# Expert lists: empty places alternate with used ones, a ring of four experts' weights, and gathers that leave out the rows of nobody

## The reference

```python
def _hier_moe(xn, w_rg, b_rg, w_re, b_re, w_gate, w_up, w_down):
    ...
    g_idx = jnp.argmax(g_logit, axis=-1)                  # one of 4 groups
    ...
    top_v, top_i = lax.top_k(e_sel, TOP_K_INNER)          # 2 of the group's 4 experts
    w_pair = jax.nn.softmax(top_v, axis=-1) * g_w
    expert_id = g_idx[..., None] * EXPERTS_PER_GROUP + top_i
    ...
    h = jax.nn.silu(jnp.einsum("btd,edf->btef", xn, w_gate)) * jnp.einsum("btd,edf->btef", xn, w_up)
    h = h * gates[..., None].astype(h.dtype)
    return jnp.einsum("btef,efd->btd", h, w_down)
```

## Time and profile before

| | us |
|---|---|
| median of the 2 runs | 1463.34 |
| lowest, highest | 1461.02, 1465.66 |
| the profiled execution | 1457.58 |
| its span (first to last instruction) | 1455.9 |
| PE busy in the span | 1147.6 (79%) |
| mean granted clock of PE | 0.887 |

### The profile page before, as it was taken

One profiled execution on the slowest core, in us unless ns is written; L12 is line 12 of the kernel. 1 busy time (PEld: TensorE's weight loads), 2 busy tenths in 40 slices (PEclk: granted clock), 3 DMA queues, 4 the chain that ended last, 5 costly groups with the idle time before them and its releaser, 6 DMA issues. The chain is left out here.

```text
span 1455.9 us, 24335 instructions
## 1 busy us (share of the span) xinstructions
PE 1147.6 (79%) x9100; PEld 866.7 (60%) x9100; DVE 574.3 (39%) x1014; ACT 468.4 (32%) x885; POOL 248.6 (17%) x290
## 2 busy tenths in 40 slices
PE   4699999498988979168687875899929979999940
PEld 3699999386877868145465554777624434444410
DVE  5320120253636455677777873212151211222231
ACT  6111010245444454467667744212100101111121
POOL 4100000000000000332323222222010221222231
PEclk9999999799898989678888887999958999999975
DMA  4402310221212020699898974932223899997567
GB/s 126 116 23 67 88 31 0 60 75 46 88 45 88 30 85 20 215 347 321 290 315 284 311 237 164 312 121 102 66 69 119 235 272 280 283 288 234 141 148 193
DMA packets 161696, 230.55 MB, mean 158 GB/s; under 512 B 15921, under 2 KB 104498, under 8 KB 161522
## 3 DMA queue, kind: packets, MB, share of 16 engines
q1 hardware_dynamic: 144962, 174.20, 36.4%
q0 software_dynamic: 13568, 49.03, 13.0%
q10 hardware_dynamic: 3072, 6.03, 1.1%
HBM read 184.13 MB, written 49.55 MB: 161 GB/s over the span
## 5 line engine op out<-in xcount | busy, mean ns | idle before, releaser
L2171 PE MATMUL ps<-ring,e_xgT 128*128 x400 | 180.7, 606 | 11.3 <-SPq L2092 10.2
L2171 PEld LDWEIGHTS ps<-ring,e_xgT 128*128 128x128 f32 x400 | 75.8, 195 | 98.9 <-issue 98.9
L634 PE MATMUL ps<-xh,a_wh 128*128 128x384 f32 (+1 forms) x288 | 101.1, 351 | 0.0
L634 PE MATMUL ps<-xl,a_wh 128*128 128x384 f32 (+1 forms) x288 | 97.1, 337 | 0.0
L634 PE MATMUL ps<-xh,a_wl 128*128 128x384 f32 (+1 forms) x288 | 96.8, 336 | 0.0
L2123 POOL DMA_INDIRECT y_rows<-e_oE,slot_to x32 | 50.5, 1579 | 254.2 <-issue 203.5
L2203 PE MATMUL ps<-ring,e_hT 128*128 x200 | 90.0, 593 | 1.0 <-DVE e_oE L2272 1.0
L2265 DVE TENSOR_TENSOR e_hid<-e_sg,ps 128x256 f32<-128x256 f32 x32 | 13.4, 420 | 180.5 <-ACT e_sg L2230 180.5
L504 DVE COPY p_vs<-ps 128x256 f32<-128x256 f32 (+1 forms) x36 | 15.3, 424 | 172.7 <-PE ps L452 172.7
L452 PE MATMUL ps<-p_wvl,xh 128*128 128x256 f32 (+1 forms) x288 | 81.3, 282 | 0.0
L452 PE MATMUL ps<-p_wvh,xl 128*128 128x256 f32 (+1 forms) x288 | 81.3, 282 | 0.0
(11 more groups left out here) (352 smaller groups left out, 2431.2 us busy)
## 6 DMA issues: line engine op xcount, KB each, us to landing
d_K<-in_cache_k SPq DMA_DIRECT2D x128, 256.0 KB, 3.9
d_V<-in_cache_v SPq DMA_DIRECT2D x128, 256.0 KB, 5.2
ring<-in_w_gate SPq DMA_DIRECT2D x16, 1024.0 KB, 7.3
ring<-in_w_up SPq DMA_DIRECT2D x16, 1024.0 KB, 11.9
ring<-in_w_down SPq DMA_DIRECT2D x16, 1024.0 KB, 13.9
zT<-a_zs POOLq DMA_DIRECT2D x12, 544.0 KB, 3.0
a_w<-in_w_in SPq DMA_DIRECT2D x12, 512.0 KB, 3.8
y_rows<-ring SPq DMA_DIRECT2D x10, 512.0 KB, 2.6
```

Of the source, the lines that this page charges most:

```text
L634: ins = pe.matmul(m.ps[:, 7, 0:w0], left[:, n % 2, k, :], right[:, k, c0:c0 + w0], start=(k == 0 and j == 0), stop=(k == KD - 1 and j == 2))
L2171: ins = pe.matmul(m.ps[:, 2 + u, :], xgT[:, u, k, :], up_k[:, bass.ds(r * KD + k, 1), :].squeeze(1), start=(k == 0), stop=(k == KD - 1))
```

## The change

**Places.** Even places and place 31 are always used; odd place 2k+1 is used only if more than 17 + k places are needed. With 25 used, places 0 to 16 are all used, then 17, 19, 21, 23, 25, 27 and 29 are empty and 18, 20, 22, 24, 26, 28, 30 and 31 used. The list positions, `tile_expert` (through `rank`) and `cum` are computed accordingly, with some more small DVE operations (`extra`, `moved`, `last`, `twice`, `rank`) and one less for the ring position.

**Ring.** RING is 4. Expert 2 is loaded near the end of mix_phase, expert 3 at the start of moe_phase. Two buffers of mix_phase that had their own space (`m_mixA`, `m_row_of` and `m_slot_of` of the second round) now lie in the ring, and the second round waits for the stores of hn.

**Gathers** from place 4 on take `slot_to` as their list with bounds_check=TOK - 1, so rows of nobody are left out.

**PE's order** is turn_x(i+1), up(i), turn_hidden(i-1), down(i-2); ACT and DVE follow. Passed-over places have waits of their own, so that their counts come in order. XR, and POOL's order, stay.

```diff
@@ -48,7 +48,8 @@
 
 
 SLOTS = (TOP * 1088 - NE) // 128 + NE
-RING = 3
+RING = 4
+ALWAYS = TOP * TOK // 128
 LEVELS = 7
 SAMPLE_LEVELS = 3
 EPS = 1e-6
@@ -1715,24 +1717,31 @@
...
-        row_of = (xT[:, :, :, :].rearrange("p u k n -> p (u k) n")[:, 0:TILES, :], sb("m_row_of", [128, TILES, 128]))
+        row_of = (xT[:, :, :, :].rearrange("p u k n -> p (u k) n")[:, 0:TILES, :],
+                  hs[:, :, :].rearrange("p u (k n) -> p (u k) n", n=128)[:, 0:TILES, :])
         slot_of = (xT[:, :, :, :].rearrange("p u k n -> p (u k n)")[:, TILES * 128:TILES * (128 + 2 * SLOTS)].rearrange(
-            "p (t c s) -> p t c s", t=TILES, c=2), sb("m_slot_of", [128, TILES, 2, SLOTS]))
+            "p (t c s) -> p t c s", t=TILES, c=2), hs[:, :, :].rearrange("p u d -> p (u d)")[
+                :, TILES * 128:TILES * (128 + 2 * SLOTS)].rearrange("p (t c s) -> p t c s", t=TILES, c=2))
         posi, posr, poss = (sb(f"m_{n}", [128, TOP, TILES], I32) for n in ("posi", "posr", "poss"))
...
@@ -1787,6 +1796,9 @@
                     if t == 0:
                         sp.wait_ge(spare_stored, 32)
                     load_x(t + 2)
+                if t == NT - 1:
+                    sp.wait_ge(mix_split, 2 * TILES)
+                    load_expert(sp, a, m, 2)
             for stored in (y_stored, hn_stored):
                 sp.wait_ge(stored[0], 16 * (TILES // 2 + 1))
                 sp.wait_ge(stored[1], 16 * (TILES // 2))
@@ -2017,6 +2032,7 @@
             do(dve.tensor_scalar(tl[:, :], tli[:, :], 1.0, None, ALU.max))
             do(dve.tensor_tensor_scan(cumf[:, :], one16[:, :], tl[:, :], 0.0, ALU.mult, ALU.add))
             do(dve.tensor_tensor(base[:, :], cumf[:, :], tl[:, :], ALU.subtract))
+            do(dve.tensor_scalar(extra[:, :], cumf[:, NE - 1:NE], float(ALWAYS), None, ALU.subtract))
             do(dve.tensor_scalar(base[:, :], base[:, :], 128.0, None, ALU.mult))
 
             do(dve.tensor_tensor(pos[:, :, :], m.ps[:, 0, 0:TILES * NE].rearrange("p (t e) -> p t e", e=NE),
@@ -2028,8 +2044,13 @@
             do(dve.tensor_copy(posi[:, :, :], posf[:, :, :]))
             do(dve.tensor_scalar(posr[:, :, :], posi[:, :, :], 127, None, ALU.bitwise_and))
             do(dve.tensor_scalar(poss[:, :, :], posi[:, :, :], 7, None, ALU.logical_shift_right))
+            do(dve.tensor_scalar(moved[:, :, :], poss[:, :, :], extra[:, :], 2.0, ALU.subtract, ALU.mult))
+            do(dve.scalar_tensor_tensor(poss[:, :, :], moved[:, :, :], float(SLOTS - 1), poss[:, :, :], ALU.min, ALU.max))
 
             for j in range(TOP):
+                if j == 1:
+                    dve.wait_ge(hn_stored[0], 16 * (TILES // 2 + 1))
+                    dve.wait_ge(hn_stored[1], 16 * (TILES // 2))
                 step(dve.tensor_tensor(row_of[j][:, :, :], within[:, :].unsqueeze(1).to_broadcast([128, TILES, 128]),
                                        posr[:, j, :].unsqueeze(2).to_broadcast([128, TILES, 128]), ALU.is_equal))
                 do(dve.tensor_tensor(slot_of[j][:, :, 0, :], slot[:, :].unsqueeze(1).to_broadcast([128, TILES, SLOTS]),
@@ -2039,17 +2060,19 @@
...
-            do(dve.tensor_copy(m.cum[:, :], cumf[0:1, :]))
-
-            do(dve.tensor_tensor(over[:, :, :], tilef[:, :].unsqueeze(2).to_broadcast([1, SLOTS, NE]),
+            do(dve.tensor_copy(m.used[:, :], cumf[0:1, NE - 1:NE]))
+            do(dve.tensor_scalar(last[:, :], cumf[0:1, :], 1.0, None, ALU.subtract))
+            do(dve.tensor_scalar(twice[:, :], last[:, :], extra[0:1, :], 2.0, ALU.subtract, ALU.mult))
+            do(dve.tensor_tensor(last[:, :], last[:, :], twice[:, :], ALU.max))
+            do(dve.tensor_scalar(m.cum[:, :], last[:, :], 1.0, None, ALU.add))
+
+            do(dve.scalar_tensor_tensor(rank[:, :], half[:, :, :].rearrange("p k j -> p (k j)")[:, 0:SLOTS], extra[0:1, :],
+                                        half_up[:, :, :].rearrange("p k j -> p (k j)")[:, 0:SLOTS], ALU.min, ALU.add))
+            do(dve.tensor_tensor(over[:, :, :], rank[:, :].unsqueeze(2).to_broadcast([1, SLOTS, NE]),
                                  cumf[0:1, :].unsqueeze(1).to_broadcast([1, SLOTS, NE]), ALU.is_ge))
             do(dve.tensor_reduce(ef[:, :], over[:, :, :], AX.X, ALU.add))
-            do(dve.tensor_scalar(ef[:, :], ef[:, :], float(NE - 1), None, ALU.min))
-            do(dve.tensor_copy(m.tile_expert[:, :], ef[:, :]))
-
-            do(dve.tensor_scalar(third[:, :], ef[:, :], 11.0, None, ALU.mult))
-            do(dve.tensor_scalar(third[:, :], third[:, :], 5, None, ALU.logical_shift_right))
-            do(dve.scalar_tensor_tensor(m.tile_ring[:, :], third[:, :], -3.0, ef[:, :], ALU.mult, ALU.add))
+            do(dve.tensor_scalar(m.tile_expert[:, :], ef[:, :], float(NE - 1), None, ALU.min))
+            do(dve.tensor_scalar(m.tile_ring[:, :], m.tile_expert[:, :], RING - 1, None, ALU.bitwise_and))
             dve.wait_ge(listed, 1)
             do(dve.tensor_scalar(m.slot_from[:, :], m.ps[:, 2, 0:SLOTS], 1.0, 0.0, ALU.subtract, ALU.max))
             do(dve.tensor_copy(someone[:, :], m.ps[:, 2, 0:SLOTS]))
@@ -2090,10 +2112,9 @@
             def landed(n):
                 sp.wait_ge(m.expert_in[n % RING], n // RING * 48 + 48)
                 sp.sem_inc(w_ready, 1)
-            load_expert(sp, a, m, 2)
-            landed(0)
-            landed(1)
-            landed(2)
+            load_expert(sp, a, m, 3)
+            for n in range(RING):
+                landed(n)
             for n in range(RING, NE):
                 done = sp.value_load(m.cum[0:1, n - RING:n - RING + 1], min_val=0, max_val=SLOTS)
                 sp.wait_ge(tile_done, done + 1)
@@ -2111,8 +2132,13 @@
             def gather(i):
                 if i >= XR:
                     pool.wait_ge(x_turned, i - XR + 1)
-                pool.indirect_dma_start(xg[:, i % XR, :], None, m.hn_rows,
-                                        bass.IndirectOffsetOnAxis(ap=m.slot_from[:, i:i + 1], axis=0)).then_inc(x_in[i % XR], 16)
+                if i < XR:
+                    pool.indirect_dma_start(xg[:, i, :], None, m.hn_rows,
+                                            bass.IndirectOffsetOnAxis(ap=m.slot_from[:, i:i + 1], axis=0)).then_inc(x_in[i], 16)
+                else:
+                    pool.indirect_dma_start(xg[:, i % XR, :], None, m.hn_rows,
+                                            bass.IndirectOffsetOnAxis(ap=m.slot_to[:, i:i + 1], axis=0),
+                                            bounds_check=TOK - 1, oob_is_err=False).then_inc(x_in[i % XR], 16)
 
             def scatter(i):
 
@@ -2151,10 +2177,10 @@
             def if_used(i, full, nothing):
 
 
-                if i < ALWAYS:
+                if i % 2 == 0 or i == SLOTS - 1:
                     full()
                 else:
-                    with pe.If(used > i):
+                    with pe.If(used > ALWAYS + i // 2):
                         full()
                     with pe.Else():
                         nothing()
@@ -2173,6 +2199,8 @@
                     ins.then_inc(up_done, 1)
 
                 def nothing():
+                    if i:
+                        pe.wait_ge(hid_ready, i)
                     pe.sem_inc(up_done, 1)
                 if_used(i, full, nothing)
 
@@ -2186,6 +2214,8 @@
                     ins.then_inc(h_turned, 1)
 
                 def unturned():
+                    if i:
+                        pe.wait_ge(ht_ready, i)
                     pe.sem_inc(h_turned, 1)
                 if_used(i, turned, unturned)
 
@@ -2215,12 +2245,13 @@
             for i in range(SLOTS):
                 if i + 1 < SLOTS:
                     turn_x(i + 1)
+                up(i)
                 if i:
                     turn_hidden(i - 1)
-                up(i)
-                if i:
-                    down(i - 1)
+                if i >= 2:
+                    down(i - 2)
             turn_hidden(SLOTS - 1)
+            down(SLOTS - 2)
             down(SLOTS - 1)
 
         @block.scalar
@@ -2241,12 +2272,13 @@
                     act.wait_ge(o_added[u], i // 2 * 16)
                 act.activation(oE[:, u, 0:512], m.ps[:, 6, :], ACT.Copy, scale=m.slot_w[:, i:i + 1]).then_inc(o_left, 1)
             for i in range(SLOTS):
+                silu(i)
                 if i:
                     hidden_out(i - 1)
-                silu(i)
-                if i:
-                    left(i - 1)
+                if i >= 2:
+                    left(i - 2)
             hidden_out(SLOTS - 1)
+            left(SLOTS - 2)
             left(SLOTS - 1)
 
         @block.vector
@@ -2275,8 +2307,9 @@
                 if i + 1 < SLOTS:
                     turn(i + 1)
                 hidden(i)
-                if i:
-                    right(i - 1)
+                if i >= 2:
+                    right(i - 2)
+            right(SLOTS - 2)
             right(SLOTS - 1)
 
 
```

(9 more changed lines are left out.)

19 lines of the change are left out of this document (11 added, 8 removed).

## The result

| | before | changed |
|---|---|---|
| median, us | 1463.34 | 1524.74 |
| lowest, highest, us | 1461.02, 1465.66 | 1523.22, 1526.27 |
| the profiled execution, us | 1457.58 | 1526.27 |
| its span, us | 1455.9 | 1524.4 |
| mean granted clock of PE | 0.887 | 0.874 |

The changed kernel is slower: ratio 1.042, 95% interval 1.034 to 1.050. The prediction had the sign and, for the pairs of an empty and a used place, the mechanism, but said 1498 us, and the time lies 5.7 us above its range of 1468 to 1519.

What follows compares the result with a forecast made beforehand. Bounds: weight waits to 1214, PE without a gap to 1399, then a 40 us tail. Place 16, place 18, five pairs, places 29 to 31, scatter and copy summed to span 1492.8, 36.9 us more; forecast 1498 us, range 1468 to 1519.

Steps and rivals of the forecast that it cites:

- the tail's fall to 8 us: Between the last down and the copy to the outputs: 40 us were to shrink to about 8.
- the pair with a real gather: Places 29 and 30, where the gather for place 31 has rows: 23.3 us, ending at 1452.7.
- The rival without waits: Gathers of empty places arrive before PE asks: 13.5 us a pair, 1443 us, 1.4% faster; chance 0.05.
- For the 13 places behind the first four I take 3 us in all, with 0 to 12 as ends.: Late gathers in places before the pairs: one used place's 11.4 us just about covers 9.6 or 12.5 us.
- the weights: Weight loads up to place 9: waits of 3, 4 and 4 us stay, plus 1.7 for a slow up.
- the first step: Up to the end of place 16 with down(14): from 1304.0 before to 1301.0.
- the second step: Empty place 17 with a real down(15), then place 18 after waiting for gather 19: down(16) ends at 1322.4.
- Sum: 3.5 + 3.8 + 2.1 + 1.7 + 6.9 + 3.4 = 21.4 us: Each empty and used pair: gather issue, landing, sequencer work, slower clock, up, down; five pairs take 107.0 us.
- the two extras that the range names: In the range only: weight loads in the first two pairs, 3 us each, and 9 us of late gathers.
- The gather of nobody: Gather for an empty place, in the pairs: 3.8 us from issue to landing; the skill's rule gave 2.0.
- Cheap gather and full clock: Rival for the pairs: empty gathers take 1.0 us and PE keeps its clock: 1469 us, +0.4%; chance 0.25.
- rows not left out: Rival: left-out rows still cost a gather, six by +2.3: 1512 us, +3.3%; chance 0.10.

Runs made afterwards that it cites:

- e1: The changed kernel with six gather buffers (XR = 6) instead of four: 1451.22 us, ratio 0.990.
- e2: The changed kernel with the earlier PE, ACT and DVE order, down one place behind up, still four gather buffers: 1444.62 us, ratio 0.986.
- e7: The changed kernel with five gather buffers (XR = 5) instead of four: 1452.52 us, ratio 0.994.
- e8: The kernel before with four ring positions and rows of nobody left out of gathers and scatters, old order and list places: 1435.61 us, ratio 0.983.
- e9: The changed kernel with 18 extra matmuls, results unused, before turn_x of odd places from 19 on: 1521.45 us, ratio 1.039.
- e6: The changed kernel with every gather by slot_from, so no row is left out: 1544.22 us, ratio 1.058.
- e3: The kernel before with the changed PE, ACT and DVE order alone, three ring positions, empty places last: 1569.86 us, ratio 1.072.

## Why the prediction had the sign and missed the size

The positions in the span, predicted and measured, give the account. "Off by" is the running difference. The sum starts from the profiled execution, 5.8 us under the median of the kernel before; between medians the forecast is 26.7 us short.

| end of | predicted | measured | off by | this step |
|---|---|---|---|---|
| place 16 (down(14)) | 1301.0 | 1315.8 | 14.8 | 14.8 |
| place 18 (down(16)) | 1322.4 | 1339.3 | 16.9 | 2.1 |
| five pairs | 1429.4 | 1461.2 | 31.8 | 14.9 |
| place 30 | 1452.7 | 1483.5 | 30.8 | -1.0 |
| last down | 1468.6 | 1500.8 | 32.2 | 1.4 |
| start of the copy | 1476.2 | 1508.5 | 32.3 | 0.1 |
| span | 1492.8 | 1524.4 | 31.6 | -0.7 |

**Right:** what bounds the pairs, in the predicted order (3.6 us to the gather's issue against 3.5, 6.87 + 3.43 for the matmuls), the tail's fall to 8 us (7.7), the slow ups in the pairs, and the pair with a real gather (22.2 us against 23.3). The rival without waits (14.8 to 16.6 us a pair in e1, against its 13.5) is a kernel that exists, but with one more gather buffer; its time, 1443 us, was nearly that of e1 and e2. The lead of POOL's queue decided it, as its last sentence said.

**The step that failed first: "For the 13 places behind the first four I take 3 us in all, with 0 to 12 as ends."** Five gathers came late, by 2.77, 2.92, 1.28, 0.33 and 1.64 us: 8.9 in all. That alone lies inside the ends. What the step left out is what a late turn_x drags along: the register reads behind it, no longer hidden (0.60, 0.29, 0.68, 0.61, 1.04: 3.2 us), and four ups at 8.64, 8.02, 8.76 and 10.16 us instead of 7.03 (7.5 us). Together 19.6 us, beyond even the upper end. In the pairs I had counted all three terms; here, for the same kind of wait, only the first. The landing of the gathers, 7.9 us in the median and 10.9 at most in this stretch, made 3.5 + 9.0 = 12.5 against 11.4 no "just about holds" but a wait wherever a load was on its way.

Against this the weights cost less than predicted: 2.85 + 0.29 and one slow up (1.8), 4.9 us against 12.7. That is no second mistake. The late gathers had already held PE back, and e1 and e7 bring the weight waits back when the gathers are in time: two waits in one stretch cover each other. The start accounts for 4.1 us (up(0) ended at 1110.2; 2.6 of them stood there when mix_phase began, and I have no cause for them; the first up took 9.28 instead of 8.14). With 16.6 more for gathers, 7.8 less for weights and 4.1 for the start, 1.9 of the first step's 14.8 us are unexplained. In the second step the sum is nearly right by luck, by other terms than its own: it waits for the gather of place 19, but that of place 18 itself came 3.56 us late, and that of place 19 in time.

**The pairs: "Sum: 3.5 + 3.8 + 2.1 + 1.7 + 6.9 + 3.4 = 21.4 us".** Measured: 27.6, 23.3, 23.5, 23.8, 23.8. From the rows of the second: 3.6 to the issue; 4.4 to the landing; from there to the up 2.7 (1374.97 to 1377.68), since a register read took 1.1; up longer by 2.2 to 2.8; 6.87 + 3.43. The terms were the right ones, and three of them short by 0.5 to 1.1 each. The first of the five, 6.2 us over the sum, is the weight load beside a gather: the load goes out at 1339.48, the gather at 1342.90, and it lands 10.1 us later, where the text had put 3 us for such pairs into the range and nothing into the sum. The forecast with the two extras that the range names, 6 us for loads in the first two pairs and 9 for late gathers, is 1513, still 12 us short.

**The gather of nobody.** I took 3.8 us from the earlier trace rows; behind a real scatter it is 4.4 to 4.8, and behind a scatter of nobody 2.1 (e8). The Trainium skill, DMA: Bandwidth & Descriptors, "Anatomy of one DMA — SWDGE (gpsimd) path", has a fixed part of about 2.0 us, and e8's 2.1 agrees. Used by itself in the pairs it would have been 2.4 us off, because there a real scatter stands ahead in the queue; the row of that situation was the better guide.

**The clock.** The Trainium skill, TensorE: Matmul & The Clock Gate, "HAM oscillation — how this bites in real kernels", describes an array that waits for a DMA again and again and restarts slowly. The trace agrees: a granted clock of 0.78 over the pairs, ups of 9.2 to 9.9 us, and single matmuls in them of up to 1217 ns where the median is 593, about half speed; e9 shows the cause by removing it.

**The rivals.** "Cheap gather and full clock" falls by the rows; "rows not left out" falls by e6, though its price, 2.3 us a gather, was near the 2.9 that e6 measured. What is not settled is the 2.6 us before mix_phase, the 1.9 us of the first step, and what e9 would give without the extra work at place 18, which was not tried.

## What to carry to other kernels

When a change puts one more place of lag between a result and its use, follow every buffer that the lagging step frees and count how many places of cover are left behind it: here two became one for gathers, which cost 80 us (e2), and with three ring positions the loads lost theirs, 57 us (e3). Then ask whether that one place can be empty. A wait at the head of a place has three costs, the wait, the sequencer's work that it uncovers, and the clock; a sum that counts them in one stage must count them in every stage.

## What the runs showed of the hardware

- A row left out of a gather is still counted as a packet (1711 more small ones), and the gather keeps its place in the queue: 2.1 us behind a scatter of nobody (e8), 4.4 to 4.8 behind a real one, 10.1 with a scatter and a weight load ahead of it, the load issued 3.4 us before.
- PE's sequencer is a resource. Reading a register mostly took 0.3 us, but 1.1 in one of the pairs; an empty place cost about 4 us of branches and reads in e8's tail, and moving the reads saved 4 us there.
- After some 9.5 us of idleness ups took 9.2 to 9.9 us; after 3.2 us of it, in e1, 7.13 in two and 8.8 in two others, and nothing in their rows tells the two kinds apart.
